# Second half of the expert up-projection: where the second one-hots of four tokens are made, and by how many instructions

## The reference, cut to what matters

```python
experts = (i1 * PEER_KEYS + i2).reshape(T, PEER_HEADS * PEER_TOPK)
gates = jax.nn.softmax(best, axis=-1)...
u = expert_u[eb]
act = jax.nn.gelu(jnp.einsum('td,tkd->tk', xb, u), approximate=False) * gb
return jnp.einsum('tk,tkd->td', act, expert_v[eb])
```

## Time and profile before

| what | value |
|---|---|
| median of three runs | 1847.3 us (1847.25 to 1850.32) |
| the profiled execution: time, span | 1850.21 us, 1848.3 us |
| PE, PEld busy | 1739.4 us (94%), 1590.8 us (86%) |
| DVE, ACT, POOL busy | 1266.9 us (69%), 962.1 us (52%), 415.7 us (22%) |
| mean granted TensorE clock | 0.977 |

### The profile page before, as it was taken

How to read it: one execution, slowest core, us unless ns; L and a number is a source line. 1 busy time by engine, 2 the same in 40 slices (tenths; PEclk the granted TensorE clock), 3 DMA queues, 4 the chain that set the end, 5 groups by cost and what they waited for, 6 DMA issues and landing times.

```text
span 1848.3 us, 36609 instructions
## 1 busy us (share of the span) xinstructions
PE 1739.4 (94%) x11651; PEld 1590.8 (86%) x11651; DVE 1266.9 (69%) x2118; ACT 962.1 (52%) x1455; POOL 415.7 (22%) x430
## 2 busy tenths in 40 slices
PE   7999999998989999999999998999899998789998
PEld 6998879998989999988888886988699998679997
DVE  5866664588976666678888887698566665556565
ACT  6653345666644444445555554654455555555554
POOL 0022300234268888810000000066000000100000
PEclk9999999999999999999999999999899999999999
DMA  5542255577764444567777777433255554135553
GB/s 182 169 137 81 74 188 182 166 211 212 214 193 163 156 157 158 166 209 240 242 242 241 241 241 247 142 119 110 100 161 183 184 189 132 35 119 187 185 181 112
DMA packets 114423, 316.59 MB, mean 171 GB/s; under 512 B 12768, under 2 KB 45920, under 8 KB 113984
## 3 DMA queue, kind: packets, MB, share of 16 engines
q1 hardware_dynamic: 113360, 311.88, 53.0%
q0 software_dynamic: 1008, 4.00, 0.7%
HBM read 296.95 MB, written 18.87 MB: 171 GB/s over the span
## 4 chain that ended last, share of the span: by engine, by line
PE 81%; DVE 10%; ACT 3%; issue 3%; POOL 2%; DMA 1%; POOLq 0%; DVEq 0%; ACTq 0%; SPq 0%
PE bank L258 13%; PE bank L260 13%; PE bank L259 13%; PE bank L319 10%; PE bank L320 10%; PE bank L321 10%; PE bank L1177 3%; DVE wlo L242 2%; POOL ylo L1462 1%; PE bank L1591 1%; PE bank L411 1%; DVE arena L1754 1%; PE bank L883 1%; ACT arena L372 1%; ACT whi L234 1%
## 5 line engine op out<-in xcount | busy, mean ns | idle before, releaser
L242 DVE TENSOR_TENSOR wlo<-raw,whi 128x1024 fp32r<-128x1024 f32 x502 | 640.1, 1277 | 199.2 <-ACT whi L234 189.5
L258 PE MATMUL bank<-xhi,whi 128*128 128x256 f32 (+1 forms) x2424 | 707.2, 292 | 15.9 <-DVE wlo L242 9.2
L260 PE MATMUL bank<-xhi,wlo 128*128 128x256 f32 (+1 forms) x2424 | 691.4, 285 | 0.0
L259 PE MATMUL bank<-xlo,whi 128*128 128x256 f32 (+1 forms) x2424 | 691.0, 285 | 0.0
L234 ACT ACTIVATE whi<-raw 128x1024 fp32r<-128x1024 f32 x524 | 550.9, 1052 | 116.1 <-PE bank L321 65.6
L258 PEld LDWEIGHTS bank<-xhi,whi 128*128 128x128 f32 x2424 | 468.1, 193 | 26.3 <-issue 13.7
L259 PEld LDWEIGHTS bank<-xlo,whi 128*128 128x128 f32 x2424 | 468.2, 193 | 1.7
L260 PEld LDWEIGHTS bank<-xhi,wlo 128*128 128x128 f32 x2424 | 467.3, 193 | 0.0
L319 PE MATMUL bank<-whi,yhi 128*128 128x512 f32 x816 | 322.2, 395 | 2.3 <-DVE ylo L1406 1.3
L320 PE MATMUL bank<-wlo,yhi 128*128 128x512 f32 x816 | 320.9, 393 | 0.0
L321 PE MATMUL bank<-whi,ylo 128*128 128x512 f32 x816 | 320.2, 392 | 0.0
(11 more groups left out here) (255 smaller groups left out, 1563.5 us busy)
## 6 DMA issues: line engine op xcount, KB each, us to landing
raw<-in_stream SPq DMA_DIRECT2D x524, 512.0 KB, 3.5
act_spill<-h SPq DMA_DIRECT2D x128, 128.0 KB, 3.2
h<-act_spill SPq DMA_DIRECT2D x128, 128.0 KB, 3.4
h<-in_x SPq DMA_DIRECT2D x1, 1024.0 KB, 5.1
arena<-in_keys POOLq DMA_DIRECT2D x1, 1024.0 KB, 5.9
h_spill<-h SPq DMA_DIRECT2D x1, 1024.0 KB, 8.5
out<-arena SPq DMA_DIRECT2D x2, 512.0 KB, 2.7
h<-h_spill POOLq DMA_DIRECT2D x2, 256.0 KB, 5.1
```

The lines of the kernel that those rows point to most:

```text
L242: nc.vector.tensor_tensor(wlo[:, q * 1024:(q + 1) * 1024], raw[:, q * 1024:(q + 1) * 1024], whi[:, q * 1024:(q + 1) * 1024].bitcast(F32), ...
L258: nc.tensor.matmul(bank[b][:, 0:T], whi[:, w], xhi[:, x], start=k == 0, stop=False)
L259: nc.tensor.matmul(bank[b][:, 0:T], whi[:, w], xlo[:, x], start=False, stop=False)
L260: last = nc.tensor.matmul(bank[b][:, 0:T], wlo[:, w], xhi[:, x], start=False, stop=k == KT - 1)
```

## The change

`HOT2` becomes two tiles, `ylo` for even steps and `yhi` for odd ones. POOL no longer takes part in the stage. DVE makes all four second one-hots of a step by one `tensor_tensor` over 128 x (4 x 128), with iota broadcast over the tokens and the numbers broadcast over the keys; it does so one step ahead, behind the fourth `one_token`. PE waits for `hot_b` once a step instead of once a token. DVE's program has 63 steps in `steps` and the last one written out.

```diff
-        PCOL = tiny[:, 12:12 + TPS]
-        HOT2 = ylo
+        HOT2 = (ylo, yhi)
...
-                    pe.wait_ge(s("hot_b"), tokens + 1)
                     if y == 0:
+                        pe.wait_ge(s("hot_b"), i * 4 + r + 1)
                         pe.wait_ge(s("g_evac"), i * 4 + r + 1)
...
-                                     HOT2[:, y * P:(y + 1) * P].bitcast(F32),
+                                     HOT2[r % 2][:, y * P:(y + 1) * P].bitcast(F32),
...
+            def four_tokens(k0, i, r):
+                n = i * (4 * TPS) + (k0 + r) * TPS
+                c4 = I2T[:, n:n + TPS] if isinstance(n, int) else I2T[:, bass.ds(n, TPS)]
+                nc.vector.tensor_tensor(HOT2[(k0 + r) % 2][:, :].rearrange("p (t k) -> p t k", k=P),
+                                        iota[:, :].unsqueeze(1).to_broadcast([P, TPS, P]),
+                                        c4.unsqueeze(2).to_broadcast([P, TPS, P]),
+                                        ALU.is_equal).then_inc(s("hot_b"), 1)
...
                 one_token(i, r, 3)
-
-            steps(dve, KEYS - E1, 4, step)
+                four_tokens(1, i, r)
+
+            four_tokens(0, 0, 0)
+            steps(dve, KEYS - E1 - 1, 4, step)
+            last = KEYS - E1 - 1
+            for y in range(TPS):
+                one_token(last // 4, last % 4, y)
+                if y == 1:
+                    split_lo(dve, N_U + KEYS - 1 + AHEAD, 0, 0, 4)
...
-            pool.wait_ge(s("cols"), 1)
-
-            def step(i, r):
-
-                n = (i * 4 + r) * TPS
-                src = I2T[:, n:n + TPS] if isinstance(n, int) else I2T[:, bass.ds(n, TPS)]
-                pool.wait_ge(s("hot_b"), n + 1)
-                pool.sem_inc(s("pool_turn"), 1)
-                nc.gpsimd.tensor_copy(PCOL, src).then_inc(s("pcol"), 1)
-                pool.wait_ge(s("pcol"), i * 4 + r + 1)
-                pool.sem_inc(s("pool_turn"), 1)
-                for y in range(TPS):
-                    pool.wait_ge(s("hot_free"), n + y + 1)
-                    pool.sem_inc(s("pool_turn"), 1)
-                    nc.gpsimd.tensor_scalar(HOT2[:, y * P:(y + 1) * P], iota[:, :], PCOL[:, y:y + 1], None,
-                                            ALU.is_equal).then_inc(s("hot_b"), 1)
-
-            pool.sem_inc(s("hot_b"), 1)
-            steps(pool, KEYS - E1, 4, step)
```

## The result

| | before | changed |
|---|---|---|
| median | 1848.57 us (1847.25 to 1850.32, 4 runs) | 1827.59 us (1823.70 to 1829.86, 4 runs) |
| profiled execution: time, span | 1850.21, 1848.3 us | 1826.62, 1824.8 us |
| first to last pair of one-hot matmuls | 259.37 us | 238.84 us |

The ratio is 0.9884, with a 95% interval of 0.9863 to 0.9904: 21.0 us less at the medians (17.7 to 25.3). The forecast was 1830 with a range of 1827 to 1838, from a gain of 17.6 us.

What follows compares the result with a forecast made beforehand. POOL was taken to set the stage's pace while PE stood still for the difference. Gains of 16.3 and 1.35 us, all else costing 0, gave 17.6 us off the 1847.3 median: 1829.7, stated as 1830, range 1827 to 1838.

Steps and rivals of the forecast that it cites:

- POOL sets the pace of the stage: POOL's work and waits fill the 16.51 us that four steps take, against 15.33 at PE's own pace.
- The arithmetic of 16 x 0.852: Per four steps, 16 POOL one-hots of 852 ns and 4 copies of 186 ns make 14.4 us; with waits, 16.6.
- Part 1: POOL leaves the stage and PE no longer waits for it: first to last pair 259.37 to 243.1 us, gain 16.3.
- the turn of PE's loop: Where PE's loop of four steps turns round, one-hot pairs are 2.17 us apart instead of 1.88, 15 times.
- Part 2: At the stage's start PE begins 1.45 us earlier, its second token 0.10 us late: gain 1.35 us.
- Part 3: DVE gets 64 compares of 128x512 at 0.68 us each, covered by its 0.40 us wait for ACT: cost 0.
- Part 4: The double HOT2 removes a wait and adds none; PE drops three of four waits for hot_b: cost 0.
- Part 5: Neighbours: ACT has room, the stream must give 171 GB/s against 159, transfers on POOL's queue wait as before: cost 0.
- the stream: Rival, 3%: the stream can't exceed this stage's 159 GB/s, a step takes 4.12 us and the time stays at 1847.
- The clock: Rival, 5%: PE's clock doesn't fall to half speed behind the stage, saving 1.6 us: 1828.1.
- The other rivals: DVE slightly late (8%, 1839), the stream as bound (3%, 1847), DVE as bound through a slow compare (4%, 1866).
- DVE a little behind: Rival, 8%: DVE's pair slips beyond 0.41 us of slack; 0.15 us a step over 64 steps costs 9.6 us: 1839.

Runs made afterwards that it cites:

- first experiment: The changed kernel, but PE waits for hot_b at every token with a value of its own, as before; 1825.92 us median, ratio 0.9877.
- the fastest version: The changed kernel with fp32r one-hots and one-hot matmuls, and DVE's step ordered tokens 0 and 1, compare, tokens 2 and 3, split_lo; 1799.17 us, ratio 0.9738.

## Why the prediction was right, and where it was off

- *POOL sets the pace of the stage*: shown. Two tiles changed nothing; taking POOL's waits on itself out of its chain gave 19.4 us between first and last pair. The arithmetic of 16 x 0.852 held for the kernel before, but 852 ns isn't POOL's price of a one-hot: it took 671 ns in the mean once the copy was ahead. The mean hangs on how long the one-hots run beside DVE's splits.
- *Part 1, 16.3 us*: 20.5 measured. The mechanism was right; the term that was mis-sized is the turn of PE's loop. "Where PE's loop of four steps turns round, they are 2.17 us apart even without a wait" took 15 x 0.29 = 4.35 us as PE's own. At 549.31 to 551.48 the pairs name no wait, but the weight load between them does (an idle 0.21 us, put down to ACT), and POOL had the last token ready only 0.02 us behind the pair's start. DVE's was done 0.45 us before it. That was enough to show the turn. With tokens early it costs nothing (first experiment, and POOL's with its copy ahead). The sum that holds is 127 distances of 1.88 us, 238.8 us, and so 20.6 us of gain. The forecast of 17.6 us lacked this term, and the measured gain is 3.4 us over it: no second error hid the first.
- *Part 2, 1.35 us*: 1.76 by the idle time (2.04 to 0.28), less 0.08 in the first distance. The 0.3 us that are left over are the idle time in front of DVE's first token ("0.30 <-issue" in the earlier trace rows), which the compare now fills: it starts while DVE ends the first half's work.
- *Part 3, compare at 0.68 us, cost 0*: 0.685 us, cost 0. The slack was taken as 0.41 us; it was some 0.8, since neighbours overlap and DVE's other instructions are shorter in the trace with POOL idle (a token 343 ns in the mean, 368 before). DVE is busy for 188 us in 530 to 770, where the forecast had 206 for the stage. 0.68 us more did no harm, 1.21 did, with 8.4 us.
- *Part 4*: right, and less than it seemed: the second tile is needed to run a step ahead, but brings nothing by itself.
- *Part 5*: 175 GB/s against 171 forecast; the stream did not hold the stage, and in the fastest version it gave 197.
- *The clock*: in the changed kernel's profile it didn't fall behind the stage (1.00 in every window), as that rival had it. It isn't the change that decides: of twelve profiles, these two and those of the ten experiments, it fell at this gap in six (mean 0.72 to 0.74 in the window from 2.5 to 8.5 us behind the last pair; the kernel before among them) and not in six (1.00; the kernel before with two tiles among them). The forecast spoke of two gaps of some 2 us; the idle time behind the stage is 1.31 us in ten of the twelve, with and without the fall. The 1.6 us that it gave for the fall can't be found in the time, since waits take them up. In the six profiles without it PE waited a second time, for 0.46 to 1.35 us, in the six with it for 0.29 us at most; and the same later matmul starts 97.04 us behind the last pair in the kernel before and 97.10 in the changed one. The Trainium skill, TensorE: Matmul & The Clock Gate, Part 1 (The HAM clock gate), has transitions come at different points from run to run; these twelve profiles agree, as far as a fall that comes or stays away behind the same gap is such a case.
- The other rivals didn't occur. What DVE a little behind costs is known now: 8.4 us at 0.13 us a step over PE's pace.

## What to carry to other kernels

An engine at 86% may be the bound of a stage: look for what its chain waits for on itself, a small copy behind the last big instruction and the next instruction behind the copy, before its work is moved elsewhere; here that small edit was worth 19.4 of the move's 20.5 us. A delay "without a named wait" at a loop's turn isn't the engine's own until the operands are known to be early, and a named one isn't shown until the program is known to wait for it: look at the rows of the weight loads too, and measure from the last operand. Whatever an in-order queue waits for should stand behind what is wanted sooner: the split before the tokens cost nothing while PE had more work, and 13 us once it had less.

## What the runs showed of the hardware that was not expected

- With the fp32 one-hot matmuls the turn of PE's loop costs nothing where the last token before it is done 0.28 us or more before its pair. Where it is late, PE's next weight load starts 0.60 to 0.65 us behind the token, against 0.27 inside the loop's body.
- One comparison of 128x512 with both inputs broadcast takes 685 ns, four `tensor_scalar`s of 128x128 take 281 each, with fp32r output; consecutive instructions of 0.34 us start 0.26 us apart.
- One-hot matmuls of 128x128 in fp32r take 0.06 us start to start where a fp32 one takes 0.11 per record and stands as two: a pair shrank from 0.45 to some 0.23 us (1.88 to 1.66 in the half step).
- POOL's one-hots, 603 ns at the median, averaged 852 ns in the kernel before and 671 with the copy ahead. Every one of over 700 ns ran beside a `split_lo` of DVE; the longest, 1740 ns, contains a whole one. Beside DVE's `one_token`s they took 621 ns, beside nothing 595. That is read from the overlaps in the traces; no run took the splits away.
